# One expert prefetch held until the first gather lands, and attention's head pairs requested one period ahead, piece by piece

## The reference, cut to what matters

```
sc = jnp.einsum('bhqd,bhkd->bhqk', qb, k).astype(jnp.float32) * scale
sc = jnp.where(kpos[None, :] <= qpos[:, None], sc, -jnp.inf)
p = jax.nn.softmax(sc, axis=-1).astype(v.dtype)
...
gate_rwkv, gate_mla = jnp.split(jax.nn.sigmoid(z_gates), N_BRANCHES, axis=-1)
merged = gate_rwkv * (y_rwkv @ w_branch[l, 0]) + gate_mla * (y_mla @ w_branch[l, 1])
x = x + gt_m[:, None, :] * (merged @ w_out[l])
...
for e in range(N_EXPERTS):
    hid = jax.nn.silu(t @ w_e_gate[e]) * (t @ w_e_up[e])
    out = out + combine[:, e:e + 1] * (hid @ w_e_down[e])
```

## Time and profile before

| | |
|---|---|
| median of 3 runs | 1557.85 us (1556.87 to 1561.06) |
| profiled execution | 1559.73 us, span of its instructions 1557.9 us |
| PE busy | 1389.4 us, 89% |
| DVE, ACT, POOL busy | 771.8, 496.2, 258.7 us |
| data moved | 246.56 MB, mean 158 GB/s |
| mean granted TensorE clock | 0.944 of 2.4 GHz |

### The profile page before, as it was taken

One profiled execution on the slowest core, in us unless ns is written; L12 is line 12 of the kernel. 1 busy time (PEld: TensorE's weight loads), 2 busy tenths in 40 slices (PEclk: granted clock), 3 DMA queues, 4 the chain that ended last, 5 costly groups with the idle time before them and its releaser, 6 DMA issues. The chain is left out here.

```text
span 1557.9 us, 32809 instructions
## 1 busy us (share of the span) xinstructions
PE 1389.4 (89%) x14293; PEld 993.7 (64%) x14293; DVE 771.8 (50%) x1122; ACT 496.2 (32%) x908; POOL 258.7 (17%) x301
## 2 busy tenths in 40 slices
PE   3799999976999998799989999999994799999990
PEld 0497777744899998577777888787884233333330
DVE  0654767656667665455557555656455112111215
ACT  1542322353334344443445444323111111111110
POOL 0001212203656552011110000000000111111110
PEclk7899999986999999899999999999996799999995
DMA  9841223261000001660003113414108699999958
GB/s 361 298 141 48 81 62 88 61 235 45 4 4 4 4 11 36 171 229 15 15 15 149 54 54 115 184 67 153 41 38 348 230 362 417 414 418 411 407 216 325
DMA packets 80828, 246.56 MB, mean 158 GB/s; under 512 B 8872, under 2 KB 42152, under 8 KB 63920
## 3 DMA queue, kind: packets, MB, share of 16 engines
q1 hardware_dynamic: 73344, 227.70, 39.4%
q0 software_dynamic: 7344, 16.79, 2.8%
HBM read 216.13 MB, written 38.29 MB: 163 GB/s over the span
## 5 line engine op out<-in xcount | busy, mean ns | idle before, releaser
L2913 PE MATMUL ps<-gu,xT 128*32 128x512 f32 x1536 | 176.9, 602 | 1.3 <-ACT xT L2994 0.7
L3102 DVE TENSOR_TENSOR sg<-sg,ps 128x256 f32<-128x256 f32 x25 | 10.5, 421 | 213.0 <-ACT sg L2999 213.0
L2913 PEld LDWEIGHTS ps<-gu,xT 128*32 128x32 f32 x1536 | 47.9, 111 | 106.8 <-issue 102.8
L351 PE MATMUL ps<-hh,wr_h 128*128 128x512 f32 x224 | 93.2, 416 | 0.5 <-DVE wr_l L347 0.5
L352 PE MATMUL ps<-hl,wr_h 128*128 128x512 f32 x224 | 88.5, 395 | 0.0
L353 PE MATMUL ps<-hh,wr_l 128*128 128x512 f32 x224 | 88.5, 395 | 0.0
L2931 PE MATMUL ps<-dn,hidT 128*32 128x512 f32 x768 | 86.8, 592 | 0.5 <-ACT hidT L3003 0.5
L2021 DVE TENSOR_REDUCE nmax<-ps 128x1 f32<-128x896 f32 (+4 forms) x64 | 45.8, 752 | 72.5 <-PE ps L1919 71.9
L1404 DVE TENSOR_TENSOR inverses<-inverses,ps 128x512 f32<-128x512 f32 (+1 forms) x80 | 49.9, 630 | 54.4 <-PE ps L1627 54.0
L1189 POOL TENSOR_TENSOR off<-mats,cst 128x256 f32<-128x256 f32 x80 | 66.4, 847 | 50.7 <-PE ps L1611 50.6
L1627 PE MATMUL ps<-inverses,xx 64*64 64x64 f32 x1280 | 71.3, 218 | 0.0
(11 more groups left out here) (419 smaller groups left out, 3339.1 us busy)
## 6 DMA issues: line engine op xcount, KB each, us to landing
gu<-w_e_gate SPq DMA_DIRECT2D x34, 1024.0 KB
gu<-w_e_up SPq DMA_DIRECT2D x34, 1024.0 KB
dn<-w_e_down SPq DMA_DIRECT2D x34, 1024.0 KB, 13.4
wbuf<-w_ada SPq DMA_DIRECT2D x16, 1024.0 KB, 11.1
wbuf<-w_ada SPq DMA_DIRECT2D x16, 512.0 KB, 5.3
wraws<-w_gates SPq DMA_DIRECT2D x16, 512.0 KB, 4.8
rows<-expert_rows SPq DMA_DIRECT2D x16, 512.0 KB, 9.4
wr<-w_rwkv SPq DMA_DIRECT2D x14, 512.0 KB, 3.6
```

Of the source, the lines that this page charges most:

```text
L351: nc.tensor.matmul(out, wt[0], mov[0], start=(k == 0), stop=False)
L2913: last = nc.tensor.matmul(ps[part, GB[b]], xT[:, b, k, part], gu[:, expert(m, c_) % WB, :, k], start=(k == 0), stop=(k == KD - 1))
```

## The change

The change has four parts, here in the order of the program.

1. `load_pair` can be called `one_by_one`: SP then waits until the queries have landed before it requests the keys, and until the keys have landed before it requests the values. Pair 0 is loaded so, in the time-mixing phase.
2. In attention, pair p (1 to 3) is requested when block 8(p - 1) + 1 is scaled, and piece by piece. The gate weights and `hraw` stay behind pair 3 in SP's list.
3. Of the experts' first weights, those of experts 3 and 4 wait on SP until the first gather has landed (`xg_in[0]`); the load of `gt` stays behind them.
4. In the overflow loop, the next turn's row transposes and their copies come last on PE and ACT.

```diff
+HELD = 3
...
-        def load_pair(sp, p):
+        def load_pair(sp, p, one_by_one=False):
...
             sp.dma_start(qT[0:QKD, two], rows_q).then_inc(pair_in[p], 16)
+            if one_by_one:
+                sp.wait_ge(pair_in[p], 16)
             sp.dma_start(kT[0:QKD, two], rows_k).then_inc(pair_in[p], 16)
+            if one_by_one:
+                sp.wait_ge(pair_in[p], 32)
             sp.dma_start(vv[:, :, two], v_dram.rearrange("p (t h n) -> p t h n", t=NT, n=N)[:, :, two])\
...
-                    load_pair(sp, 0)
+                    load_pair(sp, 0, True)
...
                         for p in range(1, HEADS // 2):
-                            load_pair(sp, p)
+                            sp.wait_ge(o_mul, NT * (p - 1) + 1)
+                            load_pair(sp, p, True)
                         gate_weights(sp, 0, 0)
...
                 for e in range(1, WB):
+                    if e == HELD:
+                        sp.wait_ge(xg_in[0], 16)
                     load_gate_up(e)
                     load_down(e)
...
                     gate_up(i)
+                    hidden_transposes(i + FIXED, 0)
+                    down(i)
                     row_transposes(i + (FIXED + 1), 0, 2 * i + (2 * FIXED + 2), i * 16 + 16 * (FIXED // XSLOTS + 2),
                                    over_gu)
-                    hidden_transposes(i + FIXED, 0)
-                    down(i)
...
                     gates(m, 0)
+                    hidden_out(m, 0)
                     rows_in(m + 1, 0)
-                    hidden_out(m, 0)
```

## The result

| | us, median | runs |
|---|---|---|
| before, same chips | 1556.87 (1553.07 to 1561.06) | 15 |
| changed | 1564.71 (1562.69 to 1568.46) | 15 |

The ratio is 1.0054 [1.0044, 1.0063], or +8.4 us (plus or minus 1.5). The forecast was 1559.4 us, with 1552.5 to 1565.5 as its range and a chance of 0.26 for slower by over 0.3%. So the time lies inside the range, but above the 1556.5 to 1562 of the forecast's own case, and on the side that was held less likely than "within 0.3%".

A forecast was written before the change was run, and what follows sets the result against it. PE, busy for 89% of the span, was taken as the bound, so transfers matter only where PE, ACT or DVE stands still. Parts 1 to 4: -3.2 + 5.6 - 0.8 + 0 = +1.6 us; forecast 1559.4, range 1552.5 to 1565.5.

The forecast's parts named there:

- the forecast's own case: Whole kernel: the main forecast, within 0.3% of the time before, own range 1556.5 to 1562 us, chance 0.56.
- the hole: Time mixing, pair 0: PE's unexplained stop of 3.76 us, read as a late code fetch, shrinks to 1.7 us; gain 2.1.
- The code fetch is not helped: Rival on pair 0 in time mixing: part 1 gives 0, the sum is +4.8, 1562.6 us; chance 0.10.
- The queries 5.6 us ... the keys have the same size and form, so 5.6: Attention, pairs in series: queries and keys 5.6 us each, values 4.2, with SP's waking up 15.6 us a pair.
- pair 1 stalls PE by 0.25 us and pair 2 by 0.65: Attention: pairs of 15.6 us miss windows of 15.35 and 14.95 us, together 0.9 us before pair 3 is requested.
- the lower bound of 4.7: Attention: least cost given for part 2, with no stall at pairs 1 and 2; centre 5.6, upper bound 10.1 us.
- Lone pieces land faster: Rival in attention: a lone piece takes 4 us, part 2 costs about 0.5, total 1554.4 us; chance 0.12.
- 2.3 us are left of 6.0: Start of expert passes: PE begins 6.0 us earlier, but late `gt` leaves 2.3; less 1.5 for the clock, gain 0.8.
- I take 2.9: Expert phase: time in us of the first gather on an empty queue, taken between 1.06 and at most 3.4.
- 6.3 MB ... about 2 us for the next gathers' 1 MB: Expert phase: traffic ahead of `gt`, 15.0 us at 420 GB/s plus about 2 for gathers; `gt` lands at 1230.3.
- Nothing; 2 us if that cover is gone.: Overflow turn: moving the row transposes, done while DVE made the hidden values, gains nothing, or 2 us without that cover.
- the side of the slower kernel: Rival in attention that pieces are slower: at 17.1 us a pair part 2 costs 10.1, kernel 1563.9 us; chance 0.13.

The follow-up runs named there:

- the run alone: One part of the change by itself, against the kernel before: part 1 0.9975, part 2 1.0010, part 3 1.0027, part 4 0.9999.

## Why the prediction came out as it did

**Part 1 was right.** Forecast -3.2 us, -2.1 from the hole and -1.1 from the clock; the traces have -3.2 and the run alone -3.9 (1.6 either way). The hole was to be 1.7 us and is 1.56 to 1.85 in the seven executions that have the part (with a second one of up to 0.9 us in some, behind it). The mechanism stands in all fourteen traces: the packet of the instruction queue is on the wire 5.4 to 6.4 us after the queries' request without the part and 4.2 to 4.4 us after it with the part, and PE goes on 2.3 to 2.9 us behind the packet in either case. The prediction had 4.4 us for the packet and 2.7 us from it to PE. "The code fetch is not helped" is out.

**Part 2 was right in its mechanism, and its size was too large.** "The queries 5.6 us ... the keys have the same size and form, so 5.6" put in the landing of queries that had keys on the queue behind them; alone they take 5.1 to 5.2, and the keys 5.0 to 5.2. So pair 3 takes 14.3 us and not 15.6, "pair 1 stalls PE by 0.25 us and pair 2 by 0.65" falls away, and after pair 3's request the weight comes 16.0 us later and not 16.9 (742.26 to 758.29): ACT stands 4.4 us for the weight and then hardly or not at all for the piece. The traces put the cost at 3.8 us, of which 3.1 are idle PE, below the lower bound of 4.7, and the run alone at 1.6 (1.4 either way). "Lone pieces land faster", which the prediction gave 0.12, was half right: 4 us would have been needed for it, and a lone piece takes 5.0 to 5.3. Its price was also worked out too low: with the second piece at 765.8 and 3.55 us from there to the exponentials they begin at 769.4, 1.4 us late and not 0.5. The Trainium skill's rule in "DMA: Bandwidth & Descriptors", section "Anatomy of one DMA", from which the prediction had estimated 3.8 us, is further from this measurement than the row was. The page gives it for DMAs that GpSimd issues, and SP issued these.

**Part 3 is the step that failed:** "2.3 us are left of 6.0", and from it "Gain: 0.8 us". `gt` was rightly named as what is late next, but it lands 28.2 us after the first gather's issue (1203.79 to DVE's start at 1232.02), and not 22.7. Two sizes were wrong. "I take 2.9" for a gather on an empty queue, when SP goes on at 4.6: the upper row gave 3.4 as "at most", but it stands for a gather whose rows were used after a busy PE, in the overflow pass, and the first one of the phase takes longer (4.5 to 4.7 us in all nine executions with held experts), for a reason that no run here shows; that is 1.7 us. And behind the release "6.3 MB ... about 2 us for the next gathers' 1 MB": between SP's release and DVE's start the DMA view counts 9.14 MB at a mean of 389 GB/s, 1.34 of them the gathers', where 7.8 at 420 were put in; that is the other 3.8 us. (SP's queue moved 7.78 MB of it, where 6.8 stood up to `gt`; the rest must be mostly expert 5's, which SP had asked for from 1222.28 on, so a load asked for later passed beside `gt`.) So PE starts 4.2 us earlier and not 6.0, stands 7.3 us and not 3.7, and is 3.7 us behind instead of 2.3 ahead. Then the clock: it was to cost 1.5 and costs 2.1 between the hidden transposes and the overflow, nearly all of it in the rows shown under part 3. +5.8 where -0.8 was forecast, 6.6 us off; the bounds ended at a loss of 0.8 and were too narrow, since on the side of a loss they varied the clock alone and held the landing of `gt` fixed. That the loss is the place of `gt`, and not the holding of the experts, is shown by the order of one request, which turns +4.2 us into -4.0.

**Part 4 was named right and priced as covered.** "Nothing; 2 us if that cover is gone." The transposes hid behind DVE's wait, as the prediction said, but were not free to move: they kept PE busy in it. In five of six executions the clock fell after the longer gap and the products took 5.1 to 5.4 us for 3.65. That is +1.5 us in the traces, which the run alone (0.9999, 2 us either way) doesn't resolve.

**The sum** was +1.6 with part 3 at its centre; with 6.6 us from part 3, 1.5 from part 4 and -1.8 from part 2 it is +7.9. None of the rivals was the cause: the side of the slower kernel was argued for the pieces, and came from `gt`. So it is luck that the time lies in the range: its upper part stood there for slower pieces and a code fetch without help, neither of which came, and the part that was priced as a gain of 0.8 us made most of the loss.

**What stays open.** The four runs alone add to +1.7 us (3.6 either way), and the four together cost 8; the traces' stretches add up, the alone times of parts 2 and 4 lie below their stretches. Likewise, leaving out part 1 changed the ratio by nothing that can be told (1.0053 for 1.0050 and 1.0054), where its stretch was 2.7 us longer (26.7 for 24.0). A part of the answer may be that single clock falls come and go between executions: attention took 171.5 to 175.0 us in kernels with the same attention, nearly all of the difference in PE's busy time, and the profiled execution of before was one of the long ones. Even ahead of the first touched place, SP asks for the queries at 614.3 to 618.6 us in the fourteen executions. Whether the parts really influence each other was not settled.

## What to carry to other kernels

When a wait is put on a queue's program order, list everything behind it and ask for the one small load that an engine needs next before the wait; here 0.5 MB on the wrong side of 6.3 MB was worth 8 us, more than all the rest. Price a request behind a released burst by all bytes that will pass before it, the gathers of other queues too, and give its landing a range of its own. Work that fills an engine's wait is not free to move away, even where nothing waits for it, and a price of a microsecond should be looked for in several traces, since one execution alone can be 2 to 3 us off in a stretch. Divide such a stretch into PE's idle and busy time: in attention, the idle time agreed within 0.3 us between the seven kernels with the same code there, where the length of the stretch scattered by 3.4 us.

## What the runs showed of the hardware

- PE's hole without a releaser in the time-mixing phase is 3.2 to 4.0 us long in the seven executions in which keys and values are asked for right behind the queries, and 1.56 to 1.85 in the seven in which they wait. The packet of the instruction queue comes 5.4 to 6.4 us after the queries' request in the first seven and 4.2 to 4.4 us after it in the others, and PE goes on 2.3 to 2.9 us behind it in all. That it carries the code which PE lacks stays an inference from these times.
- A load of 768 KB into 96 rows alone on its queue takes 5.0 to 5.3 us from issue to landing in the changed kernel; the same load with another behind it took 5.6.
- The first gather of the expert phase (128 rows of 4 KB) released PE 4.5 to 4.7 us after its issue in the nine executions in which SP's queue had been emptied, and 8.8 to 9.2 us after it in the five with a full one.
- Two short gaps of PE 1.48 us and 0.75 us long around two small transposes were followed by the 1.2 GHz level in five of six executions (down products 5.1 to 5.4 us, granted clock 0.54 to 0.58 in their first 3.6 us), and gaps of 0.40 and 0.75 in none of eight (3.65 us, clock 1.00). Which of the executions falls was not predicted by anything seen.
